# First head of the GLA branch: the value weights are split ahead of the index weights and the silu

## The reference, cut to what matters

```python
h = _rmsnorm(x, norm1_g[l]) * (1.0 + scale1) + shift1
proj = h @ w_in[l]
(gq, gk, gv, gr, glow, dq, dkv, iq, ik, iw, za, zb) = jnp.split(proj, split_points, axis=-1)
ya = _gla_branch(gq, gk, gv, gr, glow, ...) @ w_branch_a[l]
...
gate_logit = (g_low @ w_gate_up + b_gate).astype(jnp.float32)
log_alpha = jax.nn.log_sigmoid(gate_logit) / GLA_TAU
...
ada = jax.nn.silu(c) @ w_ada[l] + b_ada[l]
```

## Time and profile before

| | |
|---|---|
| median of three runs | 2174.11 us |
| the profiled execution | 2175.14 us |
| its span, first to last instruction | 2173.4 us |
| mean granted clock of TensorE in it | 0.993 |
| busy: PE / DVE / ACT / POOL | 2137.9 / 1609.3 / 967.6 / 401.8 us |
| busy share of PE, DVE, ACT, POOL | 98%, 74%, 45%, 18% |
| HBM traffic | 216 GB/s over the span |

### The profile page before, as it was taken

One profiled execution on the slowest core, in us unless ns is written; L12 is line 12 of the kernel. 1 busy time (PEld: TensorE's weight loads), 2 busy tenths in 40 slices (PEclk: granted clock), 3 DMA queues, 4 the chain that ended last, 5 costly groups with the idle time before them and its releaser, 6 DMA issues.

```text
span 2173.4 us, 30748 instructions
## 1 busy us (share of the span) xinstructions
PE 2137.9 (98%) x11787; PEld 1958.5 (90%) x11787; DVE 1609.3 (74%) x2958; ACT 967.6 (45%) x1689; POOL 401.8 (18%) x296
## 2 busy tenths in 40 slices
PE   8999989999999999999999999999999999999999
PEld 6877778887777788789999999999999999999998
DVE  4777556664976544799998897777667888888884
ACT  5444445444234423433364756766433333333333
POOL 2000110000000001000133333222223334443330
PEclk9999989999999999999999999999999999999999
DMA  7411135431231122124778888898999899999981
GB/s 257 148 50 40 49 128 192 170 136 61 104 106 41 51 85 97 64 95 146 256 279 282 307 290 284 302 314 292 333 355 385 345 375 365 370 374 376 375 334 57
DMA packets 137153, 471.07 MB, mean 217 GB/s; under 512 B 10080, under 2 KB 59488, under 8 KB 111280
## 3 DMA queue, kind: packets, MB, share of 16 engines
q1 hardware_dynamic: 45760, 283.96, 35.0%
q0 software_dynamic: 36864, 134.23, 16.4%
q10 hardware_dynamic: 54384, 50.92, 7.0%
HBM read 416.52 MB, written 52.43 MB: 216 GB/s over the span
## 4 chain that ended last, share of the span: by engine, by line
PE 84%; DVE 11%; ACTq 2%; ACT 1%; issue 1%; DMA 0%; SPq 0%; DVEq 0%
PE bank L156 83%; DVE whl L309 2%; ACTq L2235 2%; DVE L L1479 1%; DVE L L1477 1%; DVE row L2176 1%; DVE room L2120 1%; DVE room L2116 1%; PE bank L668 1%; DVE fg L2127 0%; PE bank L1568 0%; DMA XT<-in_xT 0%; DVE L L1460 0%; ACT whl L302 0%; DVE wk L1852 0%
## 5 line engine op out<-in xcount | busy, mean ns | idle before, releaser
L156 PE MATMUL bank<-xhl,whl 128*128 128x384 f32 (+1 forms) x5304 | 1092.3, 363 | 14.6 <-DVE whl L519 7.7
L156 PEld LDWEIGHTS bank<-xhl,whl 128*128 128x128 f32 x5304 | 948.9, 189 | 107.7 <-issue 11.0
L309 DVE TENSOR_TENSOR whl<-raw,whl 128x1024 fp32r<-128x1024 f32 (+2 forms) x389 | 469.1, 1215 | 254.1 <-ACT whl L302 208.5
L156 PE MATMUL bank<-ag,whl 128*128 128x384 f32 x3072 | 544.2, 340 | 1.3 <-ACT h_both L2231 1.3
L156 PEld LDWEIGHTS bank<-ag,whl 128*128 128x128 f32 x3072 | 542.1, 188 | 1.6 <-ACT h_both L2231 1.6
L302 ACT ACTIVATE whl<-raw 128x1024 fp32r<-128x1024 f32 (+2 forms) x389 | 398.0, 1034 | 217.7 <-PE bank L156 150.1
L2163 POOL DMA_INDIRECT row<-in_U_rows,row_at x128 | 182.1, 1423 | 607.6 <-DVE row L2176 432.3
L2163 POOL DMA_INDIRECT row<-in_V_rows,row_at x128 | 178.5, 1395 | 268.3 <-DVE y_tok L2192 236.3
L2192 DVE SCALAR_TENSOR_TENSOR y_tok<-row,row_a,y_tok 128x1024 f32<-128x1024 f32 x127 | 162.6, 1281 | 3.0 <-DMA row<-in_V_rows,row_at 0.3
L2176 DVE SCALAR_TENSOR_TENSOR row<-row,h_tok 128x1024 f32<-128x1024 f32 x128 | 155.7, 1218 | 0.4 <-DMA row<-in_U_rows,row_at 0.4
L156 PE MATMUL bank<-yhl,whl 128*128 128x512 f32 x540 | 132.3, 402 | 1.8 <-DVE whl L309 1.8
(11 more groups left out here) (257 smaller groups left out, 1932.2 us busy)
## 6 DMA issues: line engine op xcount, KB each, us to landing
raw<-in_U SPq DMA_DIRECT2D x64, 1024.0 KB
raw<-in_V SPq DMA_DIRECT2D x64, 1024.0 KB
hidden<-h_both ACTq DMA_DIRECT2D x32, 768.0 KB
gates<-g_stage ACTq DMA_DIRECT2D x12, 2048.0 KB, 15.0
g_ring<-gates SPq DMA_DIRECT2D x32, 768.0 KB
h_ring<-hidden SPq DMA_DIRECT2D x22, 768.0 KB, 7.8
raw<-in_w_ada SPq DMA_DIRECT2D x16, 1024.0 KB
raw<-in_w_gla SPq DMA_DIRECT2D x12, 1024.0 KB
```

Source lines behind the costliest of these rows:

```text
L156: return e.matmul(o, a, b, start=start, stop=stop, skip_group_check=True)
L309: e.tensor_tensor(lo[:, s], src[:, s], F(hi[:, s]), ALU.subtract).then_inc(dve_lo.of((i, half)))
```

## The change

In `scalar_gla` the split of `w_gla` 1 (`IT["w_gla", 0] + 1`), both halves, moves from the head of `first(0)` to right behind the copy of `ik`. The later heads keep their place. No instruction is added or taken away, and no other engine's list is touched.

```diff
             copy(e, glow[64:96, :], gla_banks.of["small"][64:96, :]).then_inc(act_gla.of("glow"))
             copy(e, ik[0:64, :], gla_banks.of["small"][0:64, :]).then_inc(act_gla.of("ik"))
+            split_hi(e, q, IT["w_gla", 0] + 1)
             q.wait_ge(pe_gla["iw"])
             e.activation(iw.rearrange("p (t h) -> p t h", t=4),
                          gla_banks.of["iw"][:, 0:P].rearrange("p (t h) -> p t h", t=4)[:, :, 16:24], ACT.Copy,
...
             def first(h):
                 E1, E2, E3, kd, ke, vtok = gla_sets[h % 2]
-                split_hi(e, q, IT["w_gla", 3 * h] + 1)
+                if h > 0:
+                    split_hi(e, q, IT["w_gla", 3 * h] + 1)
                 if h >= 2:
```

## The result

The changed kernel takes 2160.8 us in the median of seven runs (2156.18 to 2167.87); the kernel before, in seven runs, 2172.84 (2165.66 to 2174.75). The ratio is 0.995, with a 95% interval of 0.993 to 0.997.

The account below looks back on a forecast made before the run. PE, 98% busy, was taken to bound the kernel. Removed wait 5.36 plus clock 1.05 gives 6.4 us, so 2174.11 - 6.4 = 2167.7 us; range 2166.2 to 2170.5, faster by over 4.35 us at 0.82.

Parts of the forecast that it names:

- What bounds the kernel, and which wait goes: PE, 98% busy, bounds; its wait before head 0's value projection goes whole, 5.36 us.
- What the split waits for: On ACT, the moved split meets no added wait; high part done at 304.1, low part on DVE at 305.7.
- DVE, SP and ACT behind it: Later work on these engines: DVE 7.8 us earlier, `w_gla` 3 loaded in time, 2.6 us slack before head 1's query.
- the banks: Head 1's query takes a bank free at 311.0 and wanted at 320, so no new wait.
- rival A: Closer `w_gla` 3 load delays the `c` rows and silu; cost 0, still 2167.7 us; felt loss, with Rival B, 0.12.
- The clock's term, 1.05 us: Head 0's value matmuls keep the full clock without the pause: 12.83 - 11.78 = 1.05 us.
- from the span to the median: Whole-kernel time: profiled execution 2175.14, 1.03 over the median; gain subtracted from median, 2174.11 - 6.4 = 2167.7 us.
- everything behind moves by as much: Downstream of head 0's value, all engines start 6.4 us earlier and everything behind shifts equally.
- Rival B: Expert stage: one more ACT store stall reaches PE, costing 3.8 us, 2171.5 us; with felt loss from rival A, 0.12.
- Rivals C: Expert stage stores: three more stalls of 3.8 us reaching PE make the kernel slower, 2179.1 us; chance 0.03.
- D: At head 0's value, the moved split meets an unseen wait and stays late; time stays 2174.1 us; chance 0.03.
- Wrong if the clock dips although PE doesn't pause: Stated refutation sign: PE's granted clock falling without a pause; value matmuls were expected at 1.00, taking 11.8 us.

Follow-up runs that it names:

- the changed kernel with the single matmul: Changed kernel plus one extra 128x128 matmul at the head of the last stage's second group: mean 2158.0 us over 22 runs.
- the pairs with small matmuls: Kernel before and changed kernel, each with 31 extra 128x128 matmuls in the last stage (2172.1, 2165.6 us) or one (2165.4, 2158.0 us).

## Why the prediction was wrong, point by point

- **What bounds the kernel, and which wait goes:** right. The 5.3 us wait is gone, and the value follows the decay projection at once.
- **What the split waits for; DVE, SP and ACT behind it; the banks; rival A:** right, piece by piece within 0.3 us. The raw item of `w_gla` 3 came 4.7 us after its issue, as before; ACT waited 0.86 us for it and nobody waited for ACT. The silu wasn't late. The new closeness to the `c` rows cost nothing: they landed 4.1 us after their issue (4.7 before), 0.7 us behind the issue of `w_gla` 3.
- **The clock's term, 1.05 us:** right in kind, too small. I compared 12.83, up to the next query's start, with head 1's 11.78, up to its last matmul's end; like with like it is 12.83 - 11.62 = 1.2 in this execution. And one execution wasn't enough: in three others with the bare pause the value took 14.2 to 14.3. So the change wins 6.6 to 8.1 us locally (19.24 to 20.71 less 12.65), and 7.4 by the times. The Trainium skill ("TensorE: Matmul & The Clock Gate", "Part 1") says of a start at the lower clock that the count of slow matmuls differs from run to run. Here it did behind the pause, and I had allowed for it only as "somewhat less or more".
- **The step that failed** is the one from the span to the median: "That execution took 2175.14, 1.03 more than the median, which is no part of the change". I took the three runs of before, 2174.1 to 2174.75, for the kernel's time and their 0.6 us for its spread. They were three runs of the upper one of two groups that lie 9.7 us apart; the mean of its 111 runs is 2169.7. 6.4 less would have been 2163.3, and the changed kernel's 19 runs have 2162.6 in the mean. With it fell "everything behind moves by as much": the last stage has no wait of PE, and I took that for a fixed duration. A stage without waits has a spacing of its own, and busy share and clock don't show it.
- **Rival B, a stall in the expert stage that reaches PE:** its mechanism is real, and its cost is of the size that I said (3.8): between two profiles of the changed kernel with the single matmul, wait and slow matmuls together differ by 3.0 us near 1200 us and by 1.8 near 1320. But it comes and goes with and without the change and isn't a price of it. Rivals C and D didn't happen.
- **"Wrong if the clock dips although PE doesn't pause":** it never did without any pause, but once behind one so short that I hadn't thought of it. In the last profiled execution of the changed kernel with the single matmul, PE waited 0.87 us for `gate_up` ahead of the decay projection, and the value behind it ran at a mean clock of 0.87:

```profile
306.96 1.12 PE L156 MATMUL bank<-L 16*128 16x512 f32 x2 [0.87 <-DMA L<-in_gate_up]
308.01 13.27 PE L156 MATMUL bank<-whl,xhl 128*128 128x256 f32 x96
```

Had the runs of both kernels been equally divided between their two groups, the forecast of 6.4 would have been met: the groups give 5.4 and 6.2, the pairs with small matmuls 6.5 and 7.4. It was luck that made the gain look nearly double. The predicted difference was nearly right and the predicted time wasn't, since the base it was subtracted from was one of two.

## What to carry to other kernels

An engine that works through a list in order makes everything behind an early wait late: put what the bounding engine wants next in front of waits on that same engine, and look which clock the pause costs besides its own length; that price was 1.2 to 2.7 us here behind pauses of 5.3 us, and 2.3 behind one of 2.9. Before a few tenths of a per cent are forecast or believed, ask for enough runs to see whether the times fall into groups, and compare stage by stage in the profiles, since a difference in a stage that the change doesn't touch may not be the change's. A long unbroken row of equal matmuls is worth looking at by the starts of its records, and one small matmul inside it may be the cheapest gain in the kernel.

## What the runs showed of the hardware

- **Two steady spacings of the same matmuls.** 128x384 matmuls, each with its own weight load, at granted clock 1.00: 173.33 or 176.67 ns from start to start for more than 500 us, in executions of the same kernel. One 128x128 matmul within the row (some 0.2 us) turned it from wide to narrow in all four profiled executions that began wide, and none of the 91 runs with a single one inside the row reached the upper group of the kernel that it was made from. What makes an execution begin wide, no run shows. The Trainium skill ("TensorE: Matmul & The Clock Gate", "Part 1") gives columns over clock plus about 2.5 ns for back-to-back matmuls, which would be 162.5 ns for 384 columns; neither spacing is that, and the measurement decides.
- **A spacing that goes with the source of the moving columns.** In the two unbroken rows of 192 128x512 matmuls where the branches are mixed (before: from 781.7 and from 826.7 us), those that read `yhl` lie 234.3 ns apart and those that read `xhl` 226.7, and the other profiles repeat it. So this one isn't chance; that the tensor is its cause was not tested alone.
- **A store's issue can hold ACT for 9 us** when it is issued 1 to 2 us behind a 2 MB store (`gates`), which takes 15 us to land: 10.4 was the longest, 0.33 is the median, and before has no hold over 0.4 us that isn't behind such a store. How much of it reaches PE varies by up to 3 us at one place between equal executions.
- **A wait of some 2 us can bring the lower clock, and needn't.** Where PE's wait near 1320 us was 1.8 to 2.9 us long, the next 24 matmuls took 5.3 to 6.4 us in eleven profiles, with the granted clock at 0.56 over 3 us of before, and 4.4 in two (waits of 1.98 and 2.47), with 1.00 in the one of 2.47.
